# The context's norm beside the attention's output products, and four products of the first MLP ahead of the tokens' norm

## The reference, cut to what matters

```python
y, yc = attention_mixer(h, hc, ...)                 # both streams
x = x + gt1 * y
x = x + gt2 * sq_relu_mlp(rmsnorm(x, norm2_g[i]) * (1.0 + sc2) + sh2, mlp_w1[i], mlp_w2[i])
xc = xc + cgt1 * yc
xc = xc + cgt2 * sq_relu_mlp(rmsnorm(xc, norm2_g[i]) * (1.0 + csc2) + csh2, mlp_w1[i], mlp_w2[i])

def rmsnorm(x, g):
    return x * lax.rsqrt(jnp.mean(x * x, axis=-1, keepdims=True) + NORM_EPS) * g
def sq_relu_mlp(h, w1, w2):                         # w1: 1024 x 4096, w2: 4096 x 1024
    return jnp.square(jax.nn.relu(h @ w1)) @ w2
```

## Time and profile before

| | us |
|---|---|
| median of 3 runs | 3116.31 (3115.91 to 3118.94) |
| the profiled execution | 3115.32 |
| its span, first to last instruction | 3113.5 |
| PE busy | 2862.1 (92% of the span) |
| DVE busy | 1687.7 (54%) |
| ACT busy | 691.2 (22%) |

### The profile page before, as it was taken

The page is one execution under the profiler, slowest core; times in us unless marked ns, Lnnn a source line. Parts: engine busy times, 40 slices in busy tenths (PEclk is TensorE's granted clock), DMA queues, the critical chain, the costliest instruction groups (busy, mean ns, idle before and its releaser), DMA issues.

```text
span 3113.5 us, 66179 instructions
## 1 busy us (share of the span) xinstructions
PE 2862.1 (92%) x28016; PEld 2125.7 (68%) x28016; DVE 1687.7 (54%) x2919; ACT 691.2 (22%) x1336; POOL 178.4 (6%) x163
## 2 busy tenths in 40 slices
PE   7999998987999998978898999999989989997999
PEld 6877565555878565645775778744678877896984
DVE  6745443334735443433564388898655355555775
ACT  0122111111121111111344322100244323442210
POOL 0000000000000000000000000000023202430000
PEclk9999999999999999999999999999999999999999
DMA  9946999999945999999330134584320113000453
GB/s 391 385 164 274 419 420 414 420 420 394 365 148 205 392 421 420 409 421 419 120 109 1 55 114 168 200 303 162 127 69 17 44 46 115 5 4 15 165 170 112
DMA packets 99907, 702.44 MB, mean 226 GB/s; under 512 B 11376, under 2 KB 11552, under 8 KB 16912
## 3 DMA queue, kind: packets, MB, share of 16 engines
q1 hardware_dynamic: 96160, 686.52, 55.7%
q0 software_dynamic: 3440, 11.56, 1.1%
HBM read 696.98 MB, written 1.05 MB: 224 GB/s over the span
## 4 chain that ended last, share of the span: by engine, by line
PE 67%; DMA 15%; DVE 13%; ACT 3%; issue 2%; SPq 1%; DVEq 0%; POOL 0%; ACTq 0%; POOLq 0%
PE ps L229 17%; PE ps L1350 8%; PE ps L1912 8%; DMA arena<-in_w_up 6%; DVE arena L162 6%; DMA arena<-in_w_down 5%; PE ps L2786 5%; PE ps L1889 5%; PE ps L1378 4%; PE ps L2497 3%; DVE arena L166 3%; PE ps L1439 2%; ACT arena L145 2%; DMA arena<-in_mlp 2%; PE ps L2801 1%
## 5 line engine op out<-in xcount | busy, mean ns | idle before, releaser
L145 ACT ACTIVATE arena<-ps 128x256 f32<-128x256 f32 (+3 forms) x543 | 271.1, 499 | 1288.5 <-PE ps L229 238.2
L229 PE MATMUL ps<-arena 128*128 128x256 f32 x2336 | 518.8, 383 | 18.4 <-DVE arena L171 5.1
L229 PEld LDWEIGHTS ps<-arena 128*128 128x128 f32 x2336 | 443.0, 191 | 89.5 <-DVE arena L162 5.9
L162 DVE TENSOR_TENSOR arena<-arena 128x512 f32<-128x512 f32 (+6 forms) x608 | 388.7, 639 | 88.7 <-PE ps L1912 35.5
L1350 PE MATMUL ps<-arena 128*32 128x256 f32 (+2 forms) x5120 | 392.0, 391 | 45.0 <-DMA arena<-in_w_up 43.6
L1350 PEld LDWEIGHTS ps<-arena 128*32 128x32 f32 (+2 forms) x5120 | 250.5, 121 | 189.9 <-issue 101.1
L162 DVE TENSOR_TENSOR arena<-ps,arena 128x256 f32<-128x256 f32 (+3 forms) x420 | 206.7, 492 | 225.8 <-PE ps L2786 97.1
L1889 PE MATMUL ps<-arena 128*128 128x256 f32 (+1 forms) x1792 | 302.2, 331 | 8.4 <-DVE arena L171 7.8
L1889 PEld LDWEIGHTS ps<-arena 128*128 128x128 f32 x1792 | 273.5, 194 | 36.4 <-DVE arena L171 8.3
L1912 PE MATMUL ps<-arena 128*128 128x512 f32 x672 | 293.0, 593 | 2.4 <-DVE arena L162 2.2
L1378 PE MATMUL ps<-arena 128*32 128x512 f32 (+2 forms) x1280 | 205.3, 649 | 43.7 <-DMA arena<-in_w_down 43.7
(11 more groups left out here) (247 smaller groups left out, 2833.2 us busy)
## 6 DMA issues: line engine op xcount, KB each, us to landing
arena<-in_w_gate SPq DMA_DIRECT2D x128, 1024.0 KB, 18.7
arena<-in_w_up SPq DMA_DIRECT2D x128, 1024.0 KB, 19.3
arena<-in_w_down SPq DMA_DIRECT2D x128, 1024.0 KB, 19.5
arena<-in_mlp SPq DMA_DIRECT2D x80, 1024.0 KB, 4.8
arena<-in_w_ada SPq DMA_DIRECT2D x48, 1024.0 KB, 13.1
arena<-in_ada SPq DMA_DIRECT2D x48, 1024.0 KB, 6.7
arena<-in_w_in SPq DMA_DIRECT2D x30, 1024.0 KB, 11.3
arena<-in_w_rkv SPq DMA_DIRECT2D x20, 1024.0 KB, 5.0
```

Of the source, the lines that this page charges most:

```text
L145: self.e.activation(out, in_, func, bias=bias, scale=scale, **more).then_inc(*self.done(key))
L162: self.e.tensor_tensor(out, a, b, op).then_inc(*self.done(key))
L229: ins = pe.matmul(out, a, b, start=start and i == 0, stop=stop and i == len(pairs) - 1)
```

## The change

The two streams change places: half 0 of the MLP's activations is now the context and half 1 the tokens (`dst_of`, `half`, and the tests in `hidden_pe`), so that products 1 and 2 read the context alone and product 3 the tokens alone. The context's norm moves: its squares go to ACT behind the last head (`context_act`), its 8 matmuls on PE and its work on DVE stand behind output tile 1. Products 1 and 2 of rounds 0 and 1 stand ahead of the tokens' 8 matmuls against ones. The matmuls that nobody reads are 6 in place of 12. Buffers get other places.

```diff
-                    self.sq = [ctx_[:, 4096 + s * 2048:6144 + s * 2048] for s in range(2)]
+                    self.sq = [ctx_[:, 4096:6144], arena[:, 2048:4096]]
...
-                return part[:, s, :] if self.n == 256 else part
+                return part[:, 1 - s, :] if self.n == 256 else part
...
-                return self.h1[h][:, kk, :] if self.n == 256 else self.h1[0][:, kk, h * 128:h * 128 + 128]
+                return self.h1[1 - h][:, kk, :] if self.n == 256 else self.h1[0][:, kk, h * 128:h * 128 + 128]
...
+        def mlp_warm(pe, l, n):
+            b, old = psum.take(("mlp warm", l))
+            freed(pe, old)
+            keep_warm(pe, b, n)
...
-                        reach(pe, *at[("mlp", l), "normed", m.n // 256 if p == 3 else 0, 2 * j + (p != 1)])
+                        reach(pe, *at[("mlp", l), "normed", m.n // 256 if p != 3 else 0, 2 * j + (p != 1)])
...
-            eighths_pe(pe, ("mlp", l), range(nseg), m)
+            if l == 0:
+                for i in range(2):
+                    hidden_pe(pe, l, i, (1, 2))
+            eighths_pe(pe, ("mlp", l), [0], m)
+            mlp_warm(pe, l, (6, 6)[l])
             for i in range(16):
-                hidden_pe(pe, l, i)
+                hidden_pe(pe, l, i, PRODUCTS[2 * (l == 0 and i == 1):] if i else (1, 2, 3, 6, 7, 5, 4)[2 * (l == 0):])
...
-            eighths_act(act, do, ("mlp", l), l, 1, range(nseg), m, (before + " added",))
+            eighths_act(act, do, ("mlp", l), l, 1, [0], m, (before + " added",))
...
-            eighths_dve(dve, do, ("mlp", l), l, 1, range(nseg), m)
+            eighths_dve(dve, do, ("mlp", l), l, 1, [0], m)
...
             for mt in range(8):
                 projected(mt, 0)
+                if mt == 1:
+                    eighths_pe(pe, ("mlp", 0), [1], MLP[0])
...
+        def context_act(act, do):
+            m, key = MLP[0], ("mlp", 0)
+            act.wait_ge(*at["attention added", 7, "context"])
+            for k in range(8):
+                do.act(m.sq[1][:, k, :], X[1][:, k, :], ACT.Square, (key, "squared", 1, k))
+            norm_root(act, do, key, 1, m.Rs[1])
+            for k in range(1, 8, 2):
+                act.wait_ge(*at[key, "scaled", 1, k // 2])
+                do.fma(m.dst_of(1, k), m.sq[1][:, k, :], m.AB[:, 8 + k:9 + k], mv2[:, 0, 3, k, 1:2], (key, "normed", 1, k))
...
                 add_gated(do, 0, 0, mt, psum.of["attended", mt, 0], 1, ("attention added", mt))
+                if mt == 1:
+                    eighths_dve(dve, do, ("mlp", 0), 0, 1, [1], MLP[0])
```

More of the change, by code:

```diff
@@ L396, in program @@
         LATER = [(0, 5)] + [(1, v) for v in range(6)]
-        later = [[arena[:, 28872 + i * 2048 + c * 1024:29896 + i * 2048 + c * 1024] for c in range(2)] for i in range(2)]
+        later = [[arena[:, 30944 + i * 2048 + c * 1024:31968 + i * 2048 + c * 1024] for c in range(2)] for i in range(2)]
         LATER_AT = list(range(28))
@@ L1797, in __init__ @@
                     x, ring, tokens, ab, left, temps, ctx_, rs, raw1 = (
-                        arena[:, o:o + n] for o, n in ((2048, 8192), (10240, 3072), (13312, 3072), (16384, 16), (16584, 1536),
-                                                       (18120, 2048), (20168, 8192), (28360, 512), (33016, 2048)))
+                        arena[:, o:o + n] for o, n in ((2048, 8192), (10240, 3072), (13312, 3072), (30920, 16), (16584, 1536),
+                                                       (18120, 2048), (20168, 8192), (28360, 512), (28872, 2048)))
                     raw, self.h1 = [arena[:, 0:2048], raw1], [x, ctx_]
-                    self.sq = [ctx_[:, 4096 + s * 2048:6144 + s * 2048] for s in range(2)]
+                    self.sq = [ctx_[:, 4096:6144], arena[:, 2048:4096]]
                 else:
@@ L1870, in hidden_left, with hidden_pe @@
             return k[:, j, {1: 0, 2: 1, 4: 1, 7: 0}[p], {1: 0, 2: 0, 4: 1, 7: 1}[p], :]
-        def hidden_pe(pe, l, i):
+        def mlp_warm(pe, l, n):
+            b, old = psum.take(("mlp warm", l))
+            freed(pe, old)
+            keep_warm(pe, b, n)
+        def hidden_pe(pe, l, i, products=PRODUCTS):
             m = MLP[l]
[L1874 to L1877, removed]
             reach(pe, *at["mlp1", l, i])
-            for p in PRODUCTS if i else (1, 2, 3, 6, 7, 5, 4):
+            for p in products:
                 b, old = psum.take(("p", l, i, p), (FREES[p], l, i))
@@ L2318, in attention_act @@
             attend_act(act, b_heads())
+            context_act(act, do)
             end("attention", "act", acted)
```

## The result

| | us |
|---|---|
| after, median of 13 runs | 3124.86 (3116.18 to 3130.32) |
| before, median of 13 runs beside it | 3118.94 (3106.52 to 3126.56) |
| ratio | 1.0025, 95% interval 1.0014 to 1.0035 |
| the profiled execution after, span | 3123.4 |

The change makes the kernel slower by a quarter of a per cent, 7.8 us by the ratio (4.4 to 10.9); the two medians lie 5.9 us apart. Two executions far above all others are left out of the ratios of this document, one at 4840.34 us and a granted clock of 0.554, one at 3635.90 us and 0.760. The page's first line and its row of busy times: PE is as busy as before, so the time went into waits and into the clock.

What follows compares the result with a forecast made beforehand. The prediction took DVE's work to bound the seam and DVE's load loop the rounds. Before the rounds -0.1, bank wait and clock +7.5, load wait -0.3 gave +7.1 us, median 3123.4; range 3119.0 to 3126.5.

Steps and rivals of the forecast that it cites:

- The context's norm costs nothing beside the projection: Tokens' projection: nobody on PE waits for the moved norm; uncovered it would be 1.8 + 4.7 us of DVE.
- The saved half of the norm is spent on the four products ahead of the squares: Seam: 1.8 + 4.7 us saved goes into waiting for 6.9 us of products; tokens' sums at 1803.65, 0.25 later.
- Round 0: MLP's first round: product 6 at 1806.6, clock loss 1.8 us, c21 at 1815.6 against 1815.71, no gain.
- The bank wait: PE ahead of round 1's product 6: 8.9 us idle until DVE makes c11 of round 1, then 2.0 us clock loss.
- c21 of round 1 7.4 us late: Round 1's end: c21 at 1835.2 against 1827.79, after the bank wait, five products and the clock loss.
- The loop carries the delay to the end of the MLP: From round 2 on: DVE's loop of load, sums and piece starts 7.1 us later and carries that through.
- The total: Whole kernel: +7.1 us, profiled execution 3122.4, median 3123.4 (+0.23%).
- no change: Whole kernel: a difference inside about 6.2 us (0.2%); chance 0.32.
- no bank wait: Rival, round 1: wait absent or short because c11 is free earlier than read; -0.1 us, 3116.2; chance 0.07.
- PE's lead counts: Rival, rounds: the loop doesn't bind, PE ends round 1 3.6 us ahead; 3112.7, or 3110.9 with clock up; chance 0.05.

Runs made afterwards that it cites:

- without early products: The change with all products behind the tokens' squares: 0.9983 to before; with 11 unread matmuls in place of 6, 0.9975.
- c11 early: The change, but DVE makes c11 of round 1 right behind the tokens' sums, ahead of round 0's results: 0.9998 to before.
- squares first: The change with the four early products behind the tokens' squares, replacing the 6 unread matmuls: 0.9993 to before; with c11 early as well, 0.9973.
- the wait filled: The change with 18 more unread matmuls in PE's wait ahead of round 1's product 6: 1.0027 to before.
- the changed order of loads: SP loads round i + 1's weights ahead of round i's modulation piece, on the kernel before: 0.9993 to before.
- all three edits together: The change with squares first, c11 early and weights loaded ahead of the modulation piece: 0.9945 to before.
- two early products: The change with only round 0's two products ahead of the tokens' squares: 0.9993 to before.

## Why the prediction was right in its mechanism, and where its sizes were off

- *The context's norm costs nothing beside the projection*: right. PE has no wait in the projection after (1754.81 to 1785.99), and without early products the move is a gain of 6.5 to 8.1 us in place.
- *The saved half of the norm is spent on the four products ahead of the squares*: right. The tokens' sums start at 1803.73, or 1804.05 with the starts set equal (forecast 1803.65, before 1803.39). Shown by two kernels, both with c11 early, which differ in this place and in the 6 unread matmuls: +1.7 in place with products first and -8.4 with squares first. Of these 10.1 us, 6.9 are the tokens' sums (48.93 and 42.02 us behind the projection's start) and 2.1 the clock's loss in round 0, which the second kernel didn't have.
- *Round 0: c21 at 1815.6, "I take the clock's loss as before, 1.8"*: this is the term that failed. c21 came at 1816.98, 1.6 us later than before with the starts set equal and not 0.1 sooner. Product 6 started at 1806.76, 1807.08 with the starts set equal, 0.5 later than the forecast 1806.6; the half clock behind it cost 3.1 us. Both bounds that I quoted from rows, 1.8 and 2.1, were too low. It is not that PE stood idle for longer: between its cover's end and the restart it was busy for 3.75 of 7.65 us here and for 2.59 of 7.75 before. The clock stood at 0.50 for 10.2 us here (1802.7 to 1812.9) and for 6.8 before (about 1799.6 to 1806.4). The same PE work lost 2.1 us with c11 early and 3.1 with the wait filled, so the size isn't set by what PE does here; why the clock stayed down longer is open.
- *The bank wait*: right in place, releaser and length, 8.71 us (forecast 8.9). From c21 of round 0 to c11 of round 1 DVE took the 8.2 us of the sum. That it is the bank is shown by three kernels: c11 early removes it, one take fewer in between moves it by one product, no early product of round 1 removes it. The Trainium skill's rule of rotating independent groups through banks (Perfetto Trace Analysis, Matmuls), weighed in the forecast, is not contradicted: by these runs it holds as long as the evacuations stand in the order of the takes, as with c11 early.
- *c21 of round 1 7.4 us late*: 9.2 with the starts set equal. Of the 1.8 us difference the clock's 3.1 and 2.2 in place of 1.8 and 2.0 are 1.5, and the later start of product 6 of round 0 is most of the rest.
- *The loop carries the delay to the end of the MLP*: right, 9.1 us at the end of the MLP against 7.1 in the sum.
- *The total*: +7.1 us was forecast; the ratio gives 7.8 (4.4 to 10.9). The absolute 3123.4 stood on a median of three runs, 3116.31; thirteen runs put before at 3118.94, above two of the three. The measured 3124.86 is near 3123.4 in part by luck: the level was 2.6 us higher than assumed. Measured against that level, the forecast's 3123.4 is a difference of only 0.14%, inside what I had called no change: the estimate was made as a sum and should have been held as a ratio. Whether the loss is above 0.2% stays open, the interval holds both sides.
- Of the rivals, *no bank wait* (-0.1) is the kernel with c11 early, +1.7 at the MLP's end; *PE's lead counts* is refuted for this order of loads (two kernels, 0.3 us apart, one with a lead of 3.5 us); for the other order the sum above speaks for it.

## What to carry to other kernels

Work that is put ahead of its turn occupies its output bank until its reader comes to it in program order: count the takes from an early product to the one that gets its bank back, and look up what its reader stands behind. And work that fills a wait belongs behind the operation that starts the waiting chain, not ahead of it: the same four products, with c11 early in both, cost 10.1 us more ahead of the squares than behind them (2.1 of it the clock), and behind them they cost nothing against a kernel without them. A lead on the engine that is busiest gains only when the loop that feeds it has been checked for a longer period; here the changed order of loads brought 3.0 us without a lead and 6.5 with one, and all three edits together are the fastest kernel of this study, 0.55% faster than before.

## What the runs showed of the hardware that I had not expected

- The clock fell after quite short waits. Without early products PE had worked without a gap until 1804.4 and was then idle for 2.29 us; the clock went to 0.50 just after PE had started again (1.00 over 1805 to 1807, 0.62 and 0.53 in the next two windows of 2 us). In the three kernels with squares first it stayed at 1.00 through a wait of 1.60 us in the same place. Where products trickled in, as in the change, it fell while PE was still getting them in short pieces, ahead of the last wait.
- Its cost is not the same from one kernel to the next. From product 6 to c21 of round 0 (16 matmuls, 6.9 us and 0.25) five kernels lost the clock: two early products took 8.6 us, no early products 8.9, c11 early 9.3, and the change and the wait filled 10.2, a loss of 1.5, 1.7, 2.1 and 3.1. The last three do the same on PE up to there. From these rows an estimate for such a wait is 1.5 to 3 us and not a single value.
- Executions differ by much more than the three first runs showed: before ran from 3106.52 to 3126.56 in 13. In the profiles the tokens' projection, ahead of which these kernels have the same work, started between 1752.58 and 1761.71. A single profile can't be read for a few microseconds by its span. A stretch with its start set equal repeats to hundredths as long as the clock does: product 6 of round 0 starts 51.95, 51.94 and 51.94 us behind the projection in the three kernels that are alike up to there, and c21 of round 0 then differs by 0.9 us. So differences of about 1 us in place can be the clock's.
